# Routing of a mixture-of-experts layer: x1 turned in place of its norm, tiles routed inside the last output products

## The reference, cut to what matters

```
h      = x1 * rsqrt(mean(x1*x1) + EPS) * g_ffn          # one row per token
logits = h @ w_router + b_router                        # 32 experts
top_v, top_e = top_k(logits, 4);  gates = softmax(top_v)
y      = x1 + sum over the 4 chosen e of gate_e * (swiglu(h @ w_gu[e] + b_gu[e]) @ w_down[e] + b_down[e])
out    = rms_norm(y, g_final)
```

## Time and profile before

| | |
|---|---|
| median of 3 runs | 1586.99 us (1584.3 to 1587.69) |
| the profiled execution, its own time | 1584.94 us |
| its span, from first to last instruction | 1583.1 us |
| TensorE busy, of the span | 97% (1541.8 us) |
| VectorE busy | 50% (790.7 us) |
| ScalarE busy | 18% (277.6 us) |
| bytes moved by transfers | 509.52 MB, mean 322 GB/s |
| mean granted clock of TensorE | 0.987 |

### The profile page before, as it was taken

One profiled execution on the slowest core, in us unless ns is written; L12 is line 12 of the kernel. 1 busy time (PEld: TensorE's weight loads), 2 busy tenths in 40 slices (PEclk: granted clock), 3 DMA queues, 4 the chain that ended last, 5 costly groups with the idle time before them and its releaser, 6 DMA issues.

```text
span 1583.1 us, 32897 instructions
## 1 busy us (share of the span) xinstructions
PE 1541.8 (97%) x13183; PEld 713.7 (45%) x13183; DVE 790.7 (50%) x2042; ACT 277.6 (18%) x554; POOL 186.9 (12%) x269
## 2 busy tenths in 40 slices
PE   9999999999999799999999999999999999999995
PEld 8677487777755433333333333333333333333332
DVE  4349738704523645444544454445444534453448
ACT  2310020005301111111111121111111111111113
POOL 3633410014200000000000000000000000000000
PEclk9999999999999799999999999999999999999998
DMA  6555755723170599999999999999999999999995
GB/s 238 163 166 171 254 183 172 249 84 127 40 304 29 194 376 416 417 420 410 417 414 416 413 416 416 417 403 416 415 413 402 414 415 417 406 416 417 416 400 201
DMA packets 72468, 509.52 MB, mean 322 GB/s; under 512 B 13338, under 2 KB 13786, under 8 KB 47186
## 3 DMA queue, kind: packets, MB, share of 16 engines
q1 hardware_dynamic: 62154, 489.15, 77.3%
q0 software_dynamic: 10256, 19.61, 3.6%
HBM read 497.50 MB, written 19.88 MB: 327 GB/s over the span
## 4 chain that ended last, share of the span: by engine, by line
PE 77%; DMA 17%; DVE 2%; issue 1%; ACT 1%; POOL 1%; SPq 0%; DVEq 0%; POOLq 0%; ACTq 0%
PE PS L1319 36%; PE PS L935 16%; DMA weight_ring<-w_gu 16%; PE PS L1325 7%; PE PS L1243 3%; PE PS L1331 3%; PE PS L986 2%; PE PS L1051 2%; PE PS L1037 1%; PE PS L1101 1%; PE PS L1000 1%; POOL weight_ring L629 1%; DVE weight_ring L1804 1%; PE PS L1276 1%; DMA y_k<-region_x,idx_y 1%
## 5 line engine op out<-in xcount | busy, mean ns | idle before, releaser
L1319 PE MATMUL PS<-weight_ring,region_experts 128*32 128x512 f32 x5376 | 596.9, 593 | 6.7 <-DMA weight_ring<-w_gu 5.8
L1319 PEld LDWEIGHTS PS<-weight_ring,region_experts 128*32 128x32 f32 x5376 | 170.0, 110 | 400.6 <-issue 365.2
L1738 DVE TENSOR_TENSOR region_experts<-PS,region_w 128x512 f32<-128x512 f32 x96 | 66.4, 692 | 459.1 <-PE PS L1319 459.1
L1325 PE MATMUL PS<-weight_ring,act_turned 128*32 128x512 f32 x2048 | 225.6, 592 | 0.0
L935 PE MATMUL PS<-region_x,region_w 128*128 128x260 f32 (+1 forms) x928 | 209.4, 385 | 1.0 <-DVE region_x L1542 1.0
L935 PEld LDWEIGHTS PS<-region_x,region_w 128*128 128x128 f32 x928 | 175.2, 190 | 33.1 <-issue 4.6
L1729 DVE STREAM_TRANSPOSE region_experts<-region_x 32x256 f32<-32x256 f32 x372 | 161.2, 433 | 4.7
L862 ACT ACTIVATE region_experts<-region_experts 128x256 f32<-128x256 f32 x96 | 40.0, 416 | 620.8 <-DVE region_experts L1740 620.8
L1325 PEld LDWEIGHTS PS<-weight_ring,act_turned 128*32 128x32 f32 x2048 | 66.6, 110 | 153.2 <-issue 153.2
L1331 PE MATMUL PS<-weight_ring,act_turned 128*32 128x256 f32 x2048 | 118.1, 383 | 3.0 <-DVE act_turned L1750 3.0
L667 POOL DMA_INDIRECT y_k<-region_x,idx_y x32 | 30.0, 938 | 678.4 <-ACT region_x L885 602.7
(11 more groups left out here) (277 smaller groups left out, 1119.6 us busy)
## 6 DMA issues: line engine op xcount, KB each, us to landing
weight_ring<-w_gu SPq DMA_DIRECT2D x112, 2048.0 KB, 12.0
weight_ring<-w_down SPq DMA_DIRECT2D x64, 2048.0 KB, 12.3
ring_more<-w_gu SPq DMA_DIRECT2D x16, 2048.0 KB, 21.6
region_w<-w_mt SPq DMA_DIRECT2D x33, 512.0 KB, 4.2
weight_ring<-cache_kT SPq DMA_DIRECT2D x64, 256.0 KB, 4.1
weight_ring<-cache_v SPq DMA_DIRECT2D x64, 256.0 KB, 3.8
weight_ring<-w_out SPq DMA_DIRECT2D x2, 2048.0 KB, 10.8
weight_ring<-y_k SPq DMA_DIRECT2D x2, 2048.0 KB, 12.5
```

Source lines behind the costliest of these rows:

```text
L1319: mm = pe.matmul(bank(g)[GRP * q:GRP * q + GRP], hTe[u][:, k, GRP * g:GRP * g + GRP], weights(k // 2, u)[:, k % 2, SEG * q:SEG * q + SEG], ...
L1325: mm = pe.matmul(bank(3)[GRP * j:GRP * j + GRP], actT[:, kk, GRP * g:GRP * g + GRP], w_dn[:, kk, 512 * h:512 * h + 512], start=(kk == 0), ...
L1738: dve.tensor_tensor(gu, bank(g), b_wide, ALU.add).then_inc(S["biased"], 1)
```

## The change

1. **Norm weight in the router.** A column form of g_ffn is loaded with the other small things (`g_ffnT`, 4 KB, one more transfer in `small_in`), and DVE multiplies it into the router's weights once, behind the last mixer step. TensorE waits for that ahead of the first output product (`wr_scaled`). `hf_turn` turns x1 as soon as it has been added, not h. The 1/rms of a token is applied to its logits in `find`, in the step that added the bias.
2. **Order on ACT and DVE.** For the last tile ACT copies the turned tile first and then squares and sums; DVE does `find(4)` ahead of `norm_rows(4)`.
3. **Two tiles routed within the last output products.** `hf_turn(3)` and `route(2)` stand behind the first 4 products of the last tile, `route(3)` behind the first 8, and DVE's `find(2)`, `find(3)` and most of `choice_ranks` (from `gates`) run ahead of the last x1 add. `rank(0)` to `rank(3)` come right behind the last output products.
4. **Constant products.** `keep_clock` multiplies a constant tile by itself (128x128), 2, 4, 5, 5 and 12 times, behind `rank(3)`, `hf_turn(4)`, `route(4)`, `rank(4)` and `pick_rows_first`.
5. **Expert 0.** `turn_gates` and `pick_gates_first` move from ahead of expert 0 into the middle of its first round. The second round waits for `gT_done`.

```diff
@@ SP, the start
+            sp.dma_start(gffn_col, g_ffnT).then_inc(S["small_in"], 16)
             sp.dma_start(cst[:, :], consts).then_inc(S["cst_in"], 16)
-            sp.wait_ge(S["small_in"], 80)
+            sp.wait_ge(S["small_in"], 96)
@@ ACT, the loop over WO_ORDER
                 if n == NTILE - 1:
                     hfT_out(n - 1)
+                    hfT_out(n)
                 act.wait_ge(S["dve_taken"], KD + n + 1)
...
-            hfT_out(NTILE - 1)
@@ TensorE
-                pe.wait_ge(S["hf_done"], n + 1)
+                pe.wait_ge(S["dve_taken"], KD + n + 1)
                 for k in range(KD):
-                    mm = pe.transpose(PSF[:, 3072 + r * k:3072 + r * k + r], hf(t)[0:r, P * k:P * k + P], ident[0:r, 0:r])
+                    mm = pe.transpose(PSF[:, 3072 + r * k:3072 + r * k + r], xn(t)[0:r, P * k:P * k + P], ident[0:r, 0:r])
...
+            def keep_clock(times):
+                for _ in range(times):
+                    pe.matmul(bank(0, P), ones[:, :], ones[:, :], start=True, stop=True)
+
+            pe.wait_ge(S["wr_scaled"], 1)
             for n, t in enumerate(WO_ORDER):
...
-                if t < 4:
+                if n == NTILE - 1:
+                    out_half(n, 0, range(4))
+                    hf_turn(n - 1)
+                    route(n - 2)
+                    out_half(n, 0, range(4, KD))
+                    route(n - 1)
+                    mm = out_half(n, 1, range(KD))
+                elif t < 4:
                     out_half(n, 0, range(KD))
                     mm = out_half(n, 1, range(KD))
...
-                if n:
+                if 0 < n < NTILE - 1:
                     hf_turn(n - 1)
-                if n >= 2:
+                if 2 <= n < NTILE - 1:
                     route(n - 2)
-            rank(0)
-            rank(1)
-            route(NTILE - 2)
+            for n in range(NTILE - 1):
+                rank(n)
+            pe.wait_ge(S["dve_taken"], KD + NTILE - 1)
+            keep_clock(2)
             hf_turn(NTILE - 1)
+            keep_clock(4)
             route(NTILE - 1)
-            rank(2)
-            rank(3)
+            keep_clock(5)
             rank(NTILE - 1).then_inc(S["rank_ready"], 1)
+            keep_clock(5)
...
-            def pair(b, i, first=False, last=False):
+            def pair(b, i, first=False, last=False, lead=False):
...
                         mm = gu_step(0, u, k)
+                        if lead and u == 0 and k == 3:
+                            turn_gates()
+                            pick_gates_first()
                     mm.then_inc(S["round_done"], 1)
                     pick(b * SELS + e + 2, e + 1, 1 - u)
+                    if lead and u == 0:
+                        pe.wait_ge(S["gT_done"], 1)
...
                     pick_rows_first()
-                    turn_gates()
+                    keep_clock(12)
...
                 turn_rows_first(b * (NE // 2 + 1) + 1)
                 if first:
-                    pick_gates_first()
-                    pe.wait_ge(S["zero_late"], 1)
-                with pe.Fori(0, NE // 2 - 1 if first else NE // 2) as i:
+                    pair(b, 0, first, lead=True)
+                with pe.Fori(1 if first else 0, NE // 2 - 1 if first else NE // 2) as i:
                     pair(b, i, first)
@@ DVE
-                dve.tensor_tensor(rt_log[0:r, t, :], bank(4 + n % 2, NE)[0:r], rt_br[0:r], ALU.add).then_inc(S["log_taken"], 1)
+                dve.scalar_tensor_tensor(out=rt_log[0:r, t, :], in0=bank(4 + n % 2, NE)[0:r], scalar=rms[0:r, t:t + 1], in1=rt_br[0:r],
+                                         op0=ALU.mult, op1=ALU.add).then_inc(S["log_taken"], 1)
...
+            dve.tensor_tensor(wr_sb[:, :, :], wr_sb[:, :, :], gffn_col.unsqueeze(2).broadcast_to([P, KD, NE]), ALU.mult).then_inc(S["wr_scaled"], 1)
...
             for o, t in enumerate(WO_ORDER):
                 j, r = J_WO + o, TROWS[t]
+                if o == NTILE - 1:
+                    for m in (2, 3):
+                        find(m)
+                        add_before(m)
+                    choice_ranks(0, 3)
+                    choice_ranks(4, 5)
                 dve.wait_ge(S["proj_done"], j + 1)
...
+                norm(o)
+                if o == NTILE - 1:
+                    find(o)
                 norm_rows(o)
-                for m in ((), (), (0,), (1,), (2, 3))[o]:
+                for m in ((), (), (0,), (1,), ())[o]:
                     find(m)
                     add_before(m)
-            find(NTILE - 1)
             dve.wait_ge(S["rank_ready"], 1)
...
-                L(dve.scalar_tensor_tensor(out=rt_eg[:, :, 1, :], in0=rt_eq[:, :, 2, :], scalar=2.0, in1=rt_eq[:, :, 1, :],
-                                           op0=ALU.mult, op1=ALU.add))
-                L(dve.scalar_tensor_tensor(out=gx[:, :, 0:NE, 6], in0=rt_eq[:, :, 3, :], scalar=3.0, in1=rt_eg[:, :, 1, :],
-                                           op0=ALU.mult, op1=ALU.add))
+                choice_ranks(3, 4)
```

More of the change, by code:

```diff
@@ L81, in build_step @@
 def build_step(nc, xT, xnat, consts, g_mix, w_mt, w_v, w_mix, pool_scale, w_bra, w_brp, w_out,
-               w_router, b_router, b_gu, w_gu, w_down, b_down, g_ffn, g_final, bias_strip, bias_s, bias_n,
+               w_router, b_router, b_gu, w_gu, w_down, b_down, g_ffn, g_ffnT, g_final, bias_strip, bias_s, bias_n,
                cache_kT, cache_v, cache_kiT, page_table, state, stateT,
@@ L109, in build_step @@
         wr_sb = sb("wr_sb", [P, KD, NE])
-        smalls = sb("smalls", [P, 216])
+        smalls = sb("smalls", [P, 222])
         mx2 = sb("mx2", [P, 2])[:, :]
@@ L278, in build_step @@
         unused = [small(211 + n) for n in range(2)]
+        gffn_col = small(214, KD)
         top_v = part(WR, 3936, NTILE, 8)
@@ L309, in build_step @@
         ss_ready stT_in strip_in may unused_done up_full wide_done gu_free vm_in v_parts vnew_in vtail_out wblk_done
-        wiT_in wi_moved wo_in wv_in xg_done xn_in xt_ready y_ready y_rest zero_late zi_set
+        wiT_in wi_moved wo_in wr_scaled wv_in xg_done xn_in xt_ready y_ready y_rest zero_late zi_set
         zq_done sample_turned zq_zero ztmp_in y0_in ys_in ys_step ys_back zeroed dve_sum""".split()
@@ L548, in _ @@
             link(po, po.memset(wcol, 0.0), "po_step", n)
-            po.wait_ge(S["small_in"], 80)
+            po.wait_ge(S["small_in"], 96)
             for b in range(NS):
@@ L778, in _ @@
             for g in range(PG):
-                act.wait_ge(S["small_in"], 80)
+                act.wait_ge(S["small_in"], 96)
                 take(J_MIX + g, halves(pT[:, g, PAD + META:]), wide_q(J_MIX + g), scale=psc_sb[:, g:g + 1]).then_inc(S["act_taken"], 1)
@@ L1484, in _ @@
             dve.wait_ge(S["bias_in"], 16)
-            dve.wait_ge(S["small_in"], 80)
+            dve.wait_ge(S["small_in"], 96)
             for g in range(2):
@@ L1581, in _, with norm @@
                 dve.tensor_tensor(sga[:, d, META:NT], sga[:, d, META:NT], sbb[:, d, META:NT], ALU.add).then_inc(S["m_done"], 1)
-            def norm_rows(n):
+            def norm(n):
                 t = WO_ORDER[n]
@@ L1587, in norm_rows @@
                 L(dve.reciprocal(rms[0:r, t:t + 1], rms[0:r, t:t + 1]))
+            def norm_rows(n):
+                t = WO_ORDER[n]
+                r = TROWS[t]
                 dve.scalar_tensor_tensor(out=hf(t)[0:r], in0=xn(t)[0:r], scalar=rms[0:r, t:t + 1], in1=gffn[0:r],
@@ L1616, in add_before, with choice_ranks @@
                     L(dve.tensor_tensor(rt_before[:, n + 1, :], rt_before[:, n, :], m, ALU.add))
+            dve.tensor_tensor(wr_sb[:, :, :], wr_sb[:, :, :], gffn_col.unsqueeze(2).broadcast_to([P, KD, NE]), ALU.mult).then_inc(S["wr_scaled"], 1)
             dve.wait_ge(S["xn_in"], 16 * NTILE)
+            def choice_ranks(t0, t1):
+                L(dve.scalar_tensor_tensor(out=rt_eg[:, t0:t1, 1, :], in0=rt_eq[:, t0:t1, 2, :], scalar=2.0, in1=rt_eq[:, t0:t1, 1, :],
+                                           op0=ALU.mult, op1=ALU.add))
+                L(dve.scalar_tensor_tensor(out=gx[:, t0:t1, 0:NE, 6], in0=rt_eq[:, t0:t1, 3, :], scalar=3.0, in1=rt_eg[:, t0:t1, 1, :],
+                                           op0=ALU.mult, op1=ALU.add))
             for o, t in enumerate(WO_ORDER):
                 j, r = J_WO + o, TROWS[t]
+                if o == NTILE - 1:
[4 more added lines that the diff above has]
+                    choice_ranks(4, 5)
                 dve.wait_ge(S["proj_done"], j + 1)
@@ L1926 @@
         "g_ffn": x["g_ffn"][0],
+        "g_ffnT": x["g_ffn"][0].reshape(KD, P).T,
         "g_final": x["g_final"],
```

## The result

| | before | after |
|---|---|---|
| median of the runs shown | 1586.49 us (1584.3 to 1587.69) | 1596.88 us (1594.6 to 1599.22) |
| ratio | | 1.0071, 95% interval 1.0059 to 1.0084 |
| the profiled execution, its own time | 1584.94 us | 1596.15 us |
| span | 1583.1 us | 1594.0 us |

The change costs 10.4 us. I had forecast 5.3 more than before's median; the sign and the main mechanism were right, the size was too small by half. (Ratios compare fast executions alone: one execution of experiment 10 took 4150.67 us and is not in its ratio, though it is in its median of 1594.61; without it that is 1594.14.)

A forecast was written before the change was run, and what follows sets the result against it. The start of the continuous weight stream, set by expert 0's first freed slots, was taken to bound the change; 3.2 + 1.65 + 1.0 = 5.85 us later, on a base of 1586.0, gave 1591.8 us, range 1585.5 to 1595.5.

The forecast's parts named there:

- (b): Last output products: two routes and a turn moved ahead of their end cost TensorE 3.0 us.
- (d): Gather for expert 0: falls into the delayed down-weight burst, takes 10.0 us (3.8 to 10.8); expert 0 starts 3.2 later.
- (f): Expert 0's start: first products run at half clock after TensorE's wait, losing 1.0 us (0 to 1.7).
- What bounds the kernel: Between last output products and first freed slot at 556 us: any shift there moves all that follows one for one.
- (a): Ahead of the first output product: scaling the router's weights costs 0.45 us on the path (0 to 0.6).
- (c): Last tile's chain: x1 turned instead of h, find(4) at 523.9, row list ready for the gather at 528.65 us.
- (e): Expert 0's first round: gates' turning and picking between weight products cost 1.65 us (1.4 to 2.9).
- that case: Expert 0's start: the pause for the copy counts against the clock's return, up to 3.5 us at half, 1.7 lost.
- A gather slowed less: Rival: gather beside the loads takes 6.2 us, or 7.5; sum +2.05 or +3.35, time 1588.1 to 1589.4; chance 0.18.
- not at all: Rival: gather not slowed, lands in 3.8 us at 532.8; sum -0.35, time 1585.7; chance 0.12.
- the constants keep the clock: Condition of the faster rival (1582.2 us, chance 0.10): constants hold full clock over a wait under 3 us, turning 0.4 shorter.
- The rival in which the stream would make up for expert 0's lost time: Faster rival: the stream's pace sets the end, so expert 0's added products are made up; -3.85 us, 1582.2; chance 0.10.

The follow-up runs named there:

- experiment 10: Changed kernel with the router's weights scaled early: 1594.61 us, ratio 1.0063; and the combined version with 12 constants and the late scaling: 1581.26 us, ratio 0.9966.
- the repeated pair: The changed kernel and the one before, both unaltered, profiled a second time: 1596.64 against 1586.82 us, ratio 1.0062.
- experiment 5: Changed kernel with 56 constant products instead of 12 behind the row list, run twice: ratio 1.0070 and 1.0058 to the kernel before.
- 6: Changed kernel with DVE's norm_rows(4) ahead of find(4): 1596.18 against the kernel before's 1585.43 us, ratio 1.0070.
- experiment 7: Kernel before plus only the sample tile's turn and two routes within the last products, finds ahead of the x1 add: 1589.28 us, ratio 1.0025.
- the two combined ones: Changed kernel with routes behind products, gates ahead of expert 0, down weights after the gather, early scaling; 24 or 12 constants: ratio 0.9971 and 0.9970.
- experiment 1: Changed kernel with expert 0's two down-weight loads issued only when its gather has landed: 1587.18 against the kernel before's 1586.37 us, ratio 1.0009.
- experiment 3: Changed kernel with every keep_clock count at 0: 1595.89 against the kernel before's 1586.37 us, ratio 1.0060.
- before again: The kernel before, unaltered, profiled a second time; one execution, 1584.27 us.

## Why the prediction was wrong in size, point by point

The mechanism, and with it the sign, came true. What failed are three terms of the sum. The moved products of (b) were costed as if the clock stayed full, so a fall of it stood at nothing: measured 1.7 us. The gather's price in (d) was 10.0 with an upper bound of 10.8: measured 11.9. The clock at expert 0's start in (f) was 1.0: measured 2.3, above its bound of 1.7.

**What bounds the kernel.** Right in the main. The loss lies between the mixer's end and the first freed slot, and is passed on to the end: the six stages there account for 11.3 us of the profiles (13.6 in the repeated pair), the medians for 10.4 and 9.8. Through the experiments both went up and down together: against the mean of the two profiles before, the stages differ by 1.4 to 3.8 us more than the medians, except in the first run of experiment 5 and in 6 (1.6 and 0.9 less). That it is exactly one for one is not shown: the last stage was longest, 1030.0 to 1030.7, in three of the four profiles whose slots came free first (at 551.5 to 552.4).

**(a), (b) Scaling and moved routing: forecast 3.45, measured 5.5.** The two prices themselves were nearly right: 0.5 for the wait as forecast, and 3.3 for what was moved, forecast 3.0 (experiment 7). I had costed the moved products at full clock because the rows before showed them so. The failed assumption is that dense work around them keeps the clock. This grouping was made after the runs: all eleven profiles that have the late scaling, or x1 turned with the moved products, or both, hold exactly one fall of the clock within the output products, at one of the two places; the kernel before (twice), the two combined ones without the wait, and experiment 7 hold none. A fall costs 1.7 us (5.38 against 3.68 for eight records). Why experiment 7 has none, with the same small products, is open; it is a single profile. What brings the fall is so not shown, only where it was seen and what it cost.

**(c) x1 turned.** Right: 12.98 us from add to gather, forecast 12.9. The turn at 517.82 and find at 522.06 lie within 0.3 us of the forecast's places. What it gained is less sure than 17.76 - 12.98 = 4.8: against the second profile of the kernel before it is 3.1. In the combined versions it is the main part that shortens the chain, beside the later loads, and they gain; no run has it alone.

**(d) The collision: forecast 10.0 us for the gather, measured 11.9.** The mechanism was right and is shown by experiment 1: without the loads ahead of it the gather takes 3.9 us, and 9.6 of the 10.4 us are gone. The bound was too low. I took the longest of 33 gathers, 10.8, as the upper end, but all of those stand in a steady stream; here the gather was issued 3.5 us behind two whole loads, and a third (`ring_more`, 535.12) joined before it landed. Which of the two makes the difference to 10.8 no run separates; and with 3.5 to 3.6 us between them the landing was 10.2 to 12.4 in eight profiles. The rule of the Trainium skill that I weighed there ("DMA: Bandwidth & Descriptors", section "Queues, rings and completion order": turns packet by packet) gave about 6.2 us by my reckoning; every gather that was issued within 7 us of the loads took 9.2 or more, and one that was issued 11.3 us behind them took 5.0.

**(e), (f) Expert 0's first rounds: forecast 2.65, measured 4.05 and 4.5.** The gate products cost 1.72, forecast 1.65 (549.00 to 550.72). The clock cost 2.3, not 1.0: it came back not 3.5 us after the turning of the rows began at 540.97 but at 547.7, and 4.3 us of expert 0's products ran at half. TensorE stood again for 0.90 us behind the eight products of the turning; I had named that case and priced it at 1.7, and took the milder. That this pause is what delayed the clock is not shown; the first half round took from 5.34 to 6.50 us in six profiles that all have it. Experiment 5 shows that the clock would not have been at half without the standing in the wait for the gather.

The misses add up: 2.1 in (a) and (b), 1.9 in (d), 1.4 in (e) and (f), 5.4 us on top of 5.85: 11.3, the sum of the stages of the first two profiles. The medians' 10.4 is about 1 us less, within what single profiles scatter.

**The rivals.** A gather slowed less, or not at all, fell with 11.9. That the constants keep the clock was true up to the row list (no half clock from 507 to 533) and worth 0.6 us there (experiment 3), since they end 11 us too early for the wait that matters. The rival in which the stream would make up for expert 0's lost time fell too: where expert 0 lost time, the end came later.

## What to carry to other kernels

When a step is put off on an engine, look at which queue waits behind it in another: here the norm, put behind a copy on ACT and behind another DVE step, sent 4 MB of loads off 9.5 us after the x1 add instead of 4.8, while the gather came up from 17.8 to 13.0 us behind it; the gap between them shrank from 13.0 to 3.5 us, and the short transfer that the whole core was waiting for ran beside the long ones. Hold bulk loads back until the small transfer on the critical path has landed, if they have slack. And count work that fills a wait as free only while it lies in that wait: moved ahead of the wait's cause, it is paid in full.

## What the runs showed of the hardware that I had not expected

- TensorE's granted clock fell from 2.4 to 1.2 GHz with the engine busy in every microsecond (503.4 to 506.8 in the changed kernel), behind 2.4 us of transposes of 8 rows and products of 32 columns and 0.4 us of products of 512 columns; experiment 7 did work of the same shapes without a fall. It also fell when products ran again behind pauses (experiment 1: pauses until 534.76 and 536.54, fall at 536.9). A stretch at half within the output products lasted about 3.4 us and cost 1.7.
- The same kernel in two profiles has its fall at 503.4 or at 447.4, with the same 70.15 us from the products to the x1 add. The Trainium skill, "TensorE: Matmul & The Clock Gate", section "Part 1: The HAM clock gate", says of the opposite change, to the full clock at a kernel's start, that it comes at another matmul from run to run of one kernel. These traces show such scatter for the fall.
- A gather of 96 rows of 4 KB takes 3.7 to 3.9 us when the loads ahead of it are through or held back, 5.0 behind loads issued 11.3 us earlier (before again, DMA engines still 0.99 busy at its issue), 9.2 behind loads issued 6.6 us earlier, and 10.2 to 12.4 behind loads issued 3.5 us earlier.
